# Attention and recurrence scores on two 64-column strips of TensorE's array

## What is computed

```
# linear attention, per head and direction, chunk c of 64 tokens
scores = einsum('bhncd,bhnsd->bhncs', q_e, k_e)      # within a chunk
scores = where(mask, scores, 0)
o_intra = einsum('bhncs,bhnse->bhnce', scores, v)
# recurrence
f = lb + (1 - lb) * sigmoid(f_raw);  k = 1 - f
S_t = diag(f_t) S_{t-1} + k_t i_t^T;  o_t = S_t^T q_t
```

## Time and profile before

| | |
|---|---|
| median of three runs | 1459.5 us |
| the profiled execution | 1460.08 us |
| its span, first to last instruction | 1458.3 us |
| TensorE matmul busy | 1385.7 us (95%) |
| TensorE weight load busy | 1143.9 us (78%) |
| VectorE busy | 761.8 us (52%) |
| ScalarE busy | 575.7 us (39%) |
| GpSimd busy | 556.3 us (38%) |
| mean granted TensorE clock | 0.977 |

### The profile page before, as it was taken

One profiled execution on the slowest core, in us unless ns is written; L12 is line 12 of the kernel. 1 busy time (PEld: TensorE's weight loads), 2 busy tenths in 40 slices (PEclk: granted clock), 3 DMA queues, 4 the chain that ended last, 5 costly groups with the idle time before them and its releaser, 6 DMA issues.

```text
span 1458.3 us, 18620 instructions
## 1 busy us (share of the span) xinstructions
PE 1385.7 (95%) x6812; PEld 1143.9 (78%) x6812; DVE 761.8 (52%) x1223; ACT 575.7 (39%) x777; POOL 556.3 (38%) x126
## 2 busy tenths in 40 slices
PE   7899999998997999999999799997999999999997
PEld 4688888876885888888888577766888888887886
DVE  3641451655737878877521352235777777302453
ACT  6443453442334222223222445554445554334233
POOL 4232323323343434433434233224444455434341
PEclk8999999998998999999999999998999999999998
DMA  6122212223323445545333242322222211232221
GB/s 189 55 87 87 80 50 74 85 73 116 115 87 100 131 131 154 147 130 152 96 99 98 59 130 86 101 58 58 58 58 58 58 58 58 61 113 86 87 87 58
DMA packets 201599, 133.68 MB, mean 92 GB/s; under 512 B 3479, under 2 KB 197768, under 8 KB 201558
## 3 DMA queue, kind: packets, MB, share of 16 engines
q1 hardware_dynamic: 200390, 130.68, 30.5%
q10 hardware_dynamic: 848, 1.60, 0.3%
q0 software_dynamic: 320, 0.84, 0.2%
HBM read 130.99 MB, written 2.12 MB: 91 GB/s over the span
## 4 chain that ended last, share of the span: by engine, by line
issue 68%; POOL 15%; PE 14%; ACT 1%; DMA 1%; POOLq 0%; SPq 0%; ACTq 0%; DVE 0%
POOL wlo L426 15%; PE acc L441 4%; PE acc L443 3%; PE acc L442 3%; PE acc L1723 1%; DMA raw<-in_w_in_dram 1%; PE acc L1725 1%; PE acc L1724 1%; PE mid L2091 0%; ACT hhi L669 0%; PE mid L2150 0%; ACT whi L422 0%; POOLq L1696 0%; SPq L528 0%; POOL masks L1690 0%
## 5 line engine op out<-in xcount | busy, mean ns | idle before, releaser
L426 POOL TENSOR_TENSOR wlo<-raw,whi 128x2048 fp32r<-128x2048 f32 (+2 forms) x112 | 550.0, 4911 | 873.3 <-ACT whi L422 873.3
L441 PE MATMUL acc<-hhi,whi 128*128 128x512 f32 x1152 | 461.5, 401 | 18.0 <-POOL wlo L426 15.9
L442 PE MATMUL acc<-hlo,whi 128*128 128x512 f32 x1152 | 450.9, 391 | 0.0
L443 PE MATMUL acc<-hhi,wlo 128*128 128x512 f32 x1152 | 450.6, 391 | 0.0
L441 PEld LDWEIGHTS acc<-hhi,whi 128*128 128x128 f32 x1152 | 217.6, 189 | 71.2 <-POOL wlo L426 19.7
L442 PEld LDWEIGHTS acc<-hlo,whi 128*128 128x128 f32 x1152 | 217.7, 189 | 46.0 <-issue 2.9
L443 PEld LDWEIGHTS acc<-hhi,wlo 128*128 128x128 f32 x1152 | 217.4, 189 | 46.4
L422 ACT ACTIVATE whi<-raw 128x2048 fp32r<-128x2048 f32 (+2 forms) x112 | 205.7, 1836 | 58.9 <-PE acc L443 42.7
L1388 DVE TENSOR_TENSOR ada<-ada 128x512 f32<-128x512 f32 x24 | 109.1, 4545 | 0.8
L441 PE MATMUL acc<-ahi,whi 128*128 128x512 f32 x176 | 68.7, 390 | 0.0
L442 PE MATMUL acc<-alo,whi 128*128 128x512 f32 x176 | 68.5, 389 | 0.0
(11 more groups left out here) (353 smaller groups left out, 2019.1 us busy)
## 6 DMA issues: line engine op xcount, KB each, us to landing
raw<-in_w_in_dram SPq DMA_DIRECT2D x57, 512.0 KB
raw<-in_w_in_dram SPq DMA_DIRECT2D x26, 1024.0 KB
raw<-in_w_ffn_in_dram SPq DMA_DIRECT2D x44, 512.0 KB
ada<-in_w_ada_dram SPq DMA_DIRECT2D x24, 512.0 KB, 3.8
raw<-in_w_ffn_out_dram SPq DMA_DIRECT2D x16, 704.0 KB
raw<-in_w_out_dram SPq DMA_DIRECT2D x8, 1024.0 KB
xnat<-in_x_dram SPq DMA_DIRECT2D x8, 512.0 KB, 7.0
raw<-in_w_branch_gla_dram SPq DMA_DIRECT2D x4, 1024.0 KB
```

Of the source, the lines that this page charges most:

```text
L426: nc.gpsimd.tensor_tensor(wlo[:, slot, 0:n], raw[:, slot, 0:n], whi[:, slot, 0:n].bitcast(f32), ALU.subtract).then_inc(s_unit_lo, 1)
L441: nc.tensor.matmul(acc[bank][:, :], h, xh[:, k, :], start=(k == 0), stop=False)
L442: nc.tensor.matmul(acc[bank][:, :], h, xl[:, k, :], start=False, stop=False)
L443: last = nc.tensor.matmul(acc[bank][:, :], lo, xh[:, k, :], start=False, stop=(k == nk - 1))
```

## The change

The products whose result is needed only inside 64 x 64 blocks are issued block by block. A product with 64 stationary columns fills only half the array's columns; the output's partitions (0 to 63 or 64 to 127) say which half. The blocks of a tile go to the two halves in turn. `score_strips(n)` lists them. Steps 0 to 6 give two products per tile in the place of one (each with 64 key columns; 64 query columns in step 0, 32 in steps 1 to 6). Step 7 gives one product per tile (64 keys by 64 queries, always in partitions 0 to 63). In `gla_scores` each 128 x 128 product becomes two of 64 x 64. Waits, signals, masks and everything on the other engines stay.

```
+STRIP = 64
@@ gla_scores
                     for t in range(TT):
-                        ts = slice(t * P, (t + 1) * P)
-                        mm(M[2 + d][:, ts], ke[:, d, ts], qe[:, d, ts], start=True, stop=True)
+                        for c in range(2):
+                            cs = slice(t * P + c * CHUNK, t * P + (c + 1) * CHUNK)
+                            mm(M[2 + d][c * CHUNK:(c + 1) * CHUNK, cs], ke[:, d, cs], qe[:, d, cs], start=True,
+                               stop=True, skip_group_check=True)
@@ new function
+            def score_strips(n):
+
+                half = 1 << max(n - 1, 0)
+                if 2 * half <= STRIP:
+                    blocks = [slice(c, c + STRIP) for c in range(0, P, STRIP)]
+                    return [(b, b, b) for b in blocks]
+                return [(slice(c, c + half), slice(c, c + half), slice(c + half, c + 2 * half))
+                        for c in range(0, P, 2 * half)]
@@ hg_scores
                     for t in range(TT):
-                        ts = slice(t * P, (t + 1) * P)
-                        if n == 0:
-                            last = mm(M[2][:, ts], hk[:, ts], hq[:, ts], start=True, stop=True)
-                        else:
-                            last = mm(right_halves(M[(n + 2) % 4][:, ts], n - 1), hw[:, n - 1, ts],
-                                      right_halves(hw[:, n - 1, ts], n - 1), start=True, stop=True)
+                        for rows, left, right in score_strips(n):
+                            ls = slice(t * P + left.start, t * P + left.stop)
+                            rs = slice(t * P + right.start, t * P + right.stop)
+                            if n == 0:
+                                last = mm(M[2][rows, rs], hk[:, ls], hq[:, rs], start=True, stop=True,
+                                          skip_group_check=True)
+                            elif right == left:
+                                last = mm(right_halves(M[(n + 2) % 4][rows, rs], n - 1), hw[:, n - 1, ls],
+                                          right_halves(hw[:, n - 1, rs], n - 1), start=True, stop=True,
+                                          skip_group_check=True)
+                            else:
+                                last = mm(M[(n + 2) % 4][rows, rs], hw[:, n - 1, ls], hw[:, n - 1, rs], start=True,
+                                          stop=True, skip_group_check=True)
                     last.then_inc(s_h_score, 1)
```

## The result

The changed kernel took 1441.8 us (median of four runs, 1440.4 to 1444.0) beside 1458.5 us for the kernel before: a ratio of 0.9889, 95% interval 0.9877 to 0.9901. Four further runs of the same kernel gave 1440.2 us beside 1458.6, a ratio of 0.9863 (0.9847 to 0.9878). So the change is worth 16.6 to 18.4 us, where 12.9 were forecast. The first time lies 1.2 us under the forecast range. In the profiled executions the span went from 1458.3 to 1438.6 us.

A forecast was written before the change was run, and what follows sets the result against it. A loop through TensorE's scores, VectorE's masks and factors, and GpSimd bounds the recurrence. Seven intervals of 1.6 us (11.2) plus 1.75 for the eighth head give 12.9 us off 1460.08, hence 1446.6 as median; range 1443 to 1455.

The forecast's parts named there:

- The loop T0, scores, masks, states, factors, GpSimd: Recurrence: T0, the start of tile 2, waits for this circle through VectorE and GpSimd; each later T0 comes 1.6 us sooner.
- The linear attention: Its scores save 0.65 us a head, all going into TensorE's wait for `kf`; counted at 0, upper bound 2.6 us.
- the list of signs: What traces should show, such as 120 instructions a head, T0 distance 1.6 us shorter, `kf` wait 0.9 to 1.4 us.
- The price of an instruction: TensorE's narrow score products on alternating strips cost 0.038 us each; the diagonal products before cost 0.111 us.
- step 7: Recurrence scores: its eight instructions never change strips, taken at 0.5 us in sum, and are covered by the masks.
- The new wait ahead of the state products: Recurrence: TensorE's state products wait about 0.5 us for VectorE's mask of step 5, done at 1119.33.
- the distance of VectorE's memsets: Recurrence masks: without the 0.45 us wait for TensorE, later memsets stand 0.60 us apart instead of 0.89.
- The lower end of the range: 1443 us: allows the linear attention's 2.6 us and 0.1 us a head in VectorE's copies.
- The price of load and columns in turn: Rival: strips don't overlap, so each instruction pays weight load, then columns; slower, 1494 us; chance 0.03.
- That the price lands between: Rival: at 0.050 us an instruction TensorE ends last, gaining 1.1 us a head, 1451 us; chance 0.07.
- The wait that comes back: Rival, recurrence: VectorE's copies don't close up (1457.3 us), or T0 stays (1457.8 us); chance 0.07.
- The drop of the clock: Rival: half-used array and waits lower TensorE's clock to 0.50 in tile 3; 7 us slower, 1467 us; chance 0.04.

The follow-up runs named there:

- padded kernel: The changed kernel with steps 1 to 6 of the recurrence issuing five of eight strip products a second time, and step 7 all four: 1455.1 us, ratio 0.9969.

## Why the prediction was right and wrong

**Right: where the time would go.** The loop T0, scores, masks, states, factors, GpSimd held as read, and the wait for GpSimd stayed at 1.2 us a head. The linear attention gave 0 by itself; its wait for `kf` grew to 1.5 us a head in the mean and 1.7 at most, where the text had 1.45 and the list of signs 0.9 to 1.4. The price of an instruction was read off L1815 at 0.038 us with the change of width inside, and measured 0.034 in steps 1 to 6. VectorE, not TensorE, ended the masks; step 7 was covered; the clock held in the scores. The new wait ahead of the state products is 0.25 to 0.36 us in the rows, where 0.5 was put.

**Wrong: one term of the sum, the distance of VectorE's memsets.** The step was "it is the copy, 0.44 or 0.45, and the 0.15 until the next memset may start", 0.60 us, with 0.83, 0.89 and 0.89 for the first three. Measured are 0.47, and 0.82, 0.78, 0.77. From the first memset to the last it is 4.25 us against 5.01 forecast, 0.76 less. A smaller error, 0.1 us the other way, stands behind it: L1588 was put 0.47 us behind the last memset, and L1589 stands 0.58 behind it, since it still waits 0.15 us for the state products. From the transposes to L1589 it is now 1079.24 - 1072.53 = 6.71 us; it was 1122.17 - 1113.20 = 8.97. That is the 2.3 us a head. The row behind it said "0.15 <- DVE hsc L1577", and I took the name for the cause. But the distance there was 0.89 us, as at every level, and 0.89 is TensorE's eight instructions of 0.111: the pace, not the name, told who the memset waited for. The padded kernel shows this for the short copies: their distance moves with TensorE's products alone. The lower end of the range, with 0.1 us a head for the copies, was too near for the same reason: their fixed cost had never been seen without TensorE behind it.

**The arithmetic with the right term.** Seven intervals of 2.30 are 16.1 us, and after the last T0 the profiles give 212.5 less 210.4, 2.1: together 18.2. The forecast had 11.2 and 1.75. The two spans differ by 19.7; the 1.5 us on top lie ahead of the first T0 (1001.61 and 1000.15), where the strips of the linear attention had given nothing. That is within what one execution differs from another: in the second profile of the changed kernel the first T0 stands at 1003.44, and the runs of one kernel spread by 4 us and more.

**The rivals.** The price of load and columns in turn, 0.084 to 0.113 us, fell in both orders of the strips (0.031 to 0.05). That the price lands between fell too. The wait that comes back is true for the linear attention, as forecast, and false for the recurrence. The drop of the clock did not happen in the changed kernel's scores. It did for wide loads with 32 moving columns, and on strips in the first head of the kernel with one wait more on VectorE, where TensorE had stood for 3.1 us in the middle of the scores; the new waits of the changed kernel, at most 0.4 us there, bring none. The rival named the half-used array and the waits, and no run separates the two.

## What to carry to other kernels

A float32 product whose result is needed in 64-wide blocks is worth splitting if the split halves the stationary width: here 120 narrow instructions beat 64 wide ones by 2.4 us a head. The same number of instructions with half the moving columns but the full stationary width cost 100 us, most of it by the clock. Read the pace of a waiting engine before you believe the name beside its last idle time: where every step is as long as its supplier's, the floor is not in the trace, and the copy's own length (0.43 us here; 0.47 apart, 0.55 in two heads) is the better bound. When GpSimd is held behind a long unbroken run of VectorE operations, give it a gap where it is needed; one wait was worth nearly as much as the whole change.

## What the runs showed of the hardware

The narrow form is cheaper than its load suggests. A single weight load is 192 ns long at 128 columns and 138 ns at 64, a quarter less. One instruction after another costs 0.111 us at 128 columns and 0.031 to 0.038 us at 64 with 32 moving columns, a third. With 64 moving columns it is 0.031 us with the strips in turn and 0.05 on one strip. What makes up that factor is open. At 128 stationary columns, 128, 64 and 32 moving columns cost 0.117, 0.111 and 0.11 us; at 64 on one strip the moving columns do count.

TensorE's clock can fall while TensorE is never idle: it went from 1.00 to 0.50 after 4.9 to 5.8 us of 128-column loads with 32 moving columns each, with PE and PEld busy all the time. The same loads with 64 moving columns kept 1.00 for 6.2 us in the heads before the change, and the 64-column loads with 32 moving columns kept it for 3.4 us. Both lost it in a first head where TensorE had waited in the middle of the scores: the wide ones after 1.6 us (kernel before with the wait on VectorE), the narrow ones after 3.1 us. One cause for all three drops is not shown.
